# Block 2's second attention with negated scores: minima instead of maxima, and no sign change

## The reference, cut to what matters

```
scores = (q * 64 ** -0.5) @ k^T            # 128 queries a block, up to 512 local and 256 context keys
local  = where(valid, scores + bias, -1e30) # heads 0-7: a window, no bias; heads 8-15: a grid of neighbours, bias rpb
p      = softmax([sink,] context, local)    # the sink is one learned score of each head, in heads 0-7 only
out    = p @ v
```

## Time and profile before

| | us |
|---|---|
| three runs, median | 4175.17 |
| lowest, highest | 4165.76, 4179.91 |
| the profiled execution, its own time | 4163.56 |
| its span | 4161.8 |
| the paired attention, from the first `maximum` to the last diagonal product | 3487.3 to 3692.9 |
| PE, DVE, ACT, POOL busy in the span | 91%, 52%, 39%, 3% |

### The profile page before, as it was taken

How to read it: one execution, slowest core, us unless ns; L and a number is a source line. 1 busy time by engine, 2 the same in 40 slices (tenths; PEclk the granted TensorE clock), 3 DMA queues, 4 the chain that set the end, 5 groups by cost and what they waited for, 6 DMA issues and landing times.

```text
span 4161.8 us, 51828 instructions
## 1 busy us (share of the span) xinstructions
PE 3787.4 (91%) x18434; PEld 3096.5 (74%) x18434; DVE 2162.2 (52%) x3691; ACT 1602.3 (39%) x2423; POOL 137.4 (3%) x192
## 2 busy tenths in 40 slices
PE   7999988999999997999898876879999898998997
PEld 5788866877678875787577765768888677886885
DVE  4634456777653455777644555353333344755343
ACT  3233344332333344432353665442222234753222
POOL 0000000000000000000000000000000001410000
PEclk9999999999999998999898875899999999998999
DMA  3212323456221231345513300011212121112332
GB/s 120 91 61 81 106 66 101 144 153 202 71 87 60 90 113 51 122 146 172 159 46 68 30 0 0 26 41 61 66 61 65 45 66 45 19 45 66 96 96 71
DMA packets 114225, 333.81 MB, mean 80 GB/s; under 512 B 34479, under 2 KB 35247, under 8 KB 113455
## 3 DMA queue, kind: packets, MB, share of 16 engines
q1 hardware_dynamic: 83087, 269.06, 21.4%
q0 software_dynamic: 14400, 52.44, 4.2%
q10 hardware_dynamic: 16608, 10.61, 1.0%
HBM read 329.97 MB, written 6.97 MB: 81 GB/s over the span
## 4 chain that ended last, share of the span: by engine, by line
PE 80%; DVE 9%; ACT 5%; issue 2%; DVEq 2%; DMA 1%; POOL 1%; ACTq 0%; SPq 0%
PE PS L437 13%; PE PS L438 12%; PE PS L439 12%; PE PS L787 10%; PE PS L788 10%; PE PS L790 10%; PE PS L487 2%; PE PS L575 2%; PE PS L897 2%; PE PS L917 1%; PE PS L891 1%; PE PS L832 1%; PE PS L584 1%; PE PS L852 1%; DVE HVAL L1726 1%
## 5 line engine op out<-in xcount | busy, mean ns | idle before, releaser
L1682 DVE TENSOR_TENSOR WL<-RAW,WH 128x1024 fp32r<-128x1024 f32 x494 | 604.4, 1224 | 537.2 <-ACT WH L1082 533.4
L1082 ACT ACTIVATE WH<-RAW 128x1024 fp32r<-128x1024 f32 x494 | 521.3, 1055 | 680.3 <-PE PS L790 363.4
L437 PE MATMUL PS<-HHI,WH 128*128 128x512 f32 x1632 | 656.9, 403 | 42.2 <-DVE HLO L1719 37.0
L438 PE MATMUL PS<-HLO,WH 128*128 128x512 f32 x1632 | 643.7, 394 | 0.0
L439 PE MATMUL PS<-HHI,WL 128*128 128x512 f32 x1632 | 643.2, 394 | 0.0
L787 PE MATMUL PS<-H2HI,WH 128*128 128x512 f32 (+1 forms) x1464 | 525.7, 359 | 45.6 <-DVE H2LO L2131 35.8
L788 PE MATMUL PS<-H2LO,WH 128*128 128x512 f32 (+1 forms) x1464 | 496.1, 355 | 0.0
L790 PE MATMUL PS<-H2HI,WL 128*128 128x512 f32 (+1 forms) x1464 | 429.2, 354 | 0.0
L437 PEld LDWEIGHTS PS<-HHI,WH 128*128 128x128 f32 x1632 | 309.6, 190 | 131.2 <-issue 47.1
L787 PEld LDWEIGHTS PS<-H2HI,WH 128*128 128x128 f32 x1464 | 278.7, 190 | 120.5 <-issue 38.9
L439 PEld LDWEIGHTS PS<-HHI,WL 128*128 128x128 f32 x1632 | 309.8, 190 | 71.5
(11 more groups left out here) (333 smaller groups left out, 6266.0 us busy)
## 6 DMA issues: line engine op xcount, KB each, us to landing
RAW<-in_stream SPq DMA_DIRECT2D x494, 512.0 KB, 3.5
MODW<-in_modw POOLq DMA_DIRECT2D x96, 512.0 KB, 4.0
bias_rows<-in_rpb SPq DMA_DIRECT2D x1, 4762.5 KB, 55.0
MEM<-in_mem ACTq DMA_DIRECT2D x3, 1024.0 KB, 4.9
X<-in_x SPq DMA_DIRECT2D x1, 2048.0 KB, 9.3
CROW<-in_crow POOLq DMA_DIRECT2D x4, 512.0 KB, 4.5
out<-X SPq DMA_DIRECT2D x1, 2048.0 KB, 7.3
BIAS<-bias_rows ACTq DMA_DIRECT2D x8, 224.0 KB, 4.7
```

The lines of the kernel that those rows point to most:

```text
L437: nc.tensor.matmul(out, WH[:, slot, b * P:(b + 1) * P], hi, start=start, stop=False)
L438: nc.tensor.matmul(out, WH[:, slot, b * P:(b + 1) * P], lo, start=False, stop=False)
L1082: A(WH[:, d, :], RAW[:, s, :], ACT.Copy).then_inc(high_split, 1)
L1682: TT(WL[:, d, :], RAW[:, s, :], WH[:, d, :].bitcast(F32), ALU.subtract).then_inc(split_ready, 1)
```

## The change

Scores are carried with their sign changed. The queries of the last layer are scaled by -(64 ** -0.5) instead of 64 ** -0.5; the masks hold +1e30 for a forbidden key; the biases are subtracted from the mask where the mask was added to them; `maximum` takes minima, and starts from a negated sink (a new tile of 8 columns, filled once in block 2's prologue) or from +1e30; the exponential has the scale -1. The minimum of the negated scores is already what `exps` needs as bias, so the second `TTR` writes it where line 2199 wrote, line 2199 is gone, and the `drain` behind the second `TTR` now carries the semaphore. The instructions of the first block and of the first layer are as they were.

```diff
+        SINK = place2("SINK", [P, 8])
...
-                    nc.gpsimd.tensor_tensor(b, b, CMASK[:].unsqueeze(1).to_broadcast([P, DR, HD]), ALU.add).then_inc(grid_ready, 1)
+                    nc.gpsimd.tensor_tensor(b, CMASK[:].unsqueeze(1).to_broadcast([P, DR, HD]), b, ALU.subtract).then_inc(grid_ready, 1)
...
-                A(dst, FLAT[:, 3 * p * T:3 * p * T + TA].unsqueeze(1), ACT.Identity if scale else ACT.Copy, scale=HD ** -0.5 if scale else 1.0).then_inc(taken[p], 1)
+                A(dst, FLAT[:, 3 * p * T:3 * p * T + TA].unsqueeze(1), ACT.Identity if scale else ACT.Copy, scale=scale or 1.0).then_inc(taken[p], 1)
...
-                    A(p, p, ACT.Exp, bias=MX[:, 2 + h:3 + h], accum_out=DEN[:, h:h + 1]).then_inc(pair_exp, 1)
+                    A(p, p, ACT.Exp, bias=MX[:, 2 + h:3 + h], scale=-1.0, accum_out=DEN[:, h:h + 1]).then_inc(pair_exp, 1)
...
+            TS(SINK[:], SM[:, 4 * HD:4 * HD + 8], -1.0, None, ALU.mult)
             dve.drain().then_inc(lam_ready, 1)
...
-                        added, least = BAND[:, c:c + n - TC], SM[:, 4 * HD + j + 4 * h:4 * HD + j + 4 * h + 1]
+                        added, least = BAND[:, c:c + n - TC], SINK[:, j + 4 * h:j + 4 * h + 1]
...
-                    TTR(p[:, 0:n - TC], FLAT[:, c0:c0 + n - TC], added, 1.0, least, ALU.add, ALU.max, MX[:, 0:1])
+                    TTR(p[:, 0:n - TC], FLAT[:, c0:c0 + n - TC], added, 1.0, least, ALU.add, ALU.min, MX[:, h:h + 1])
                     dve.drain()
-                    TTR(p[:, n - TC:n], FLAT[:, c0 + T:c0 + T + TC], ZERO[:], 1.0, MX[:, 0:1], ALU.add, ALU.max, MX[:, 1:2])
-                    dve.drain()
-                    TS(MX[:, 2 + h:3 + h], MX[:, 1:2], -1.0, None, ALU.mult).then_inc(pair_max, 1)
+                    TTR(p[:, n - TC:n], FLAT[:, c0 + T:c0 + T + TC], ZERO[:], 1.0, MX[:, h:h + 1], ALU.add, ALU.min, MX[:, 2 + h:3 + h])
+                    dve.drain().then_inc(pair_max, 1)
...
-    band = np.concatenate([np.where(abs(jj - 3 * P - i) <= 128, 0, NEG), np.where((ck >= cs) & (ck < cs + 16), 0, NEG)], axis=1).astype(f4)
+    band = np.concatenate([np.where(abs(jj - 3 * P - i) <= 128, 0, -NEG), np.where((ck >= cs) & (ck < cs + 16), 0, -NEG)], axis=1).astype(f4)
```

More of the change, by code:

```diff
@@ L1603, in _ @@
                 for t, c in enumerate(IN_ORDER):
-                    take2(U2[:, c, :].unsqueeze(1), l and c in Q_CHUNK)
+                    take2(U2[:, c, :].unsqueeze(1), -HD ** -0.5 if l and c in Q_CHUNK else None)
                     if l == 0 and 3 <= t < 8:
@@ L2186, in maximum @@
                         c = (3 - qb + local[0]) * P
-                        added, least = BAND[:, c:c + n - TC], SM[:, 4 * HD + j + 4 * h:4 * HD + j + 4 * h + 1]
+                        added, least = BAND[:, c:c + n - TC], SINK[:, j + 4 * h:j + 4 * h + 1]
                     else:
-                        added, least = GRID_BIAS[j % 2][h][:, (6 - 2 * qb) * HD:(6 - 2 * qb) * HD + T], NEG
+                        added, least = GRID_BIAS[j % 2][h][:, (6 - 2 * qb) * HD:(6 - 2 * qb) * HD + T], -NEG
                         if qb == 0:
```

## The result

| | median us | lowest, highest | runs |
|---|---|---|---|
| before | 4170.82 | 4163.06, 4182.19 | 13 |
| after | 4187.80 | 4175.42, 4195.21 | 13 |

The ratio after to before is 1.0038 (95% interval 1.0027 to 1.0049): 17 us slower where 1.3 us faster, in effect no change, was forecast. The forecast set out from the median of three runs, 4175.17 us, 4.35 us above that of 13; from 4170.82 its sum would have given 4169.5, further off. The profiled execution of the changed kernel took 4188.95 us.

The account below looks back on a forecast made before the run. The prediction had PE bounding most of the span and the order of waits deciding the window half; -0.9 - 0.4 - 0.07 + 0.07 = -1.3 us, from 4163.56 to 4162.3, or 4173.9 against the median; range 4162 to 4183.

Parts of the forecast that it names:

- The rest: Outside the attention's main terms: minima, changed constants and the 32-byte move at 0, the negated sink's instruction at 0.07 us.
- Rival 4: The 32 bytes or the shift in time move something unseen by over 0.3% either way: 4160 or 4188; chance 0.09.
- The window half: Paired attention's band pairs, 3512 to 3588 us: 13 sign changes in the chain at 0.07 us each, 0.9 us gained.
- The ring: One band pair's chain: head 1's exponential, `inverse`, next `maximum`, line 2199, `turned_low`, `turned`, back to the exponential; 5.87 us a turn.
- The queue's wait: Ahead of `turned_low` in the band half: if line 2199's 0.07 us is this wait, which stays, the gain is 0.
- rival 1: Full latencies count: 0.15 us at 13 turns, another 0.15 for ACT's earlier start, 0.5 at the start; 4170.8 us, chance 0.14.
- The first pairs: Start of the paired attention, each sign change in series: 0.07 + 2 x 0.15 = 0.4 us gained (0.2 to 0.5).
- POOL's block: After the first pairs, POOL's mask additions hold DVE's one-column addition 1.59 us, so the next two visits gain nothing.
- The grid half: Paired attention, 3588 to 3693 us: PE decides, line 2199 is in the chain once, in the last pair; 0.07 us gained.
- rival 3: POOL pays for the repeated operand in first place at three places in the chain: 4186.3 us, chance 0.03.
- sink instruction: Added behind line 2095 of the prologue to negate the sink: costs 0.07 us (0 to 0.15).
- The distance over the stage: From the first `maximum` to the last diagonal product of the paired attention: 205.6 us, forecast to become 204.3.

Follow-up runs that it names:

- pad8: The kernel before plus an unused tile of 8 columns (32 bytes) where the change put its own: 4187.76 us against 4169.90, ratio 1.0042.
- after64: The changed kernel with its new tile made 64 columns wide (8 used): 4164.59 us against 4170.46 for the kernel before, ratio 0.9984.
- pad16: The kernel before plus an unused tile of 16 columns (64 bytes) where the change put its own: ratio 1.0035.
- pad56: The kernel before plus an unused tile of 56 columns (224 bytes) where the change put its own: ratio 1.0034.
- weights16: The kernel before with the weight tiles moved on by 64 bytes and everything behind them by 128: 4204.18 us, ratio 1.0076.
- all8: The kernel before with its whole memory, weights included, moved on by 32 bytes: ratio 1.0000.
- g_only: The kernel before with only GHI, GLO and Y2, the tiles of the MLP's second half, moved on by 32 bytes: 4176.00 us, ratio 1.0013.
- pad48: The kernel before plus an unused tile of 48 columns (192 bytes) where the change put its own: ratio 1.0010.

## Why the prediction was wrong

**The step that failed** stands in "The rest": "The new tile moves all that lies behind it in block 2 by 32 bytes; no row shows whether an address matters, and I take 0." It measured 17.9 us by itself (pad8), and it is the whole result. Rival 4 named it and gave it a chance of 0.09, with the right size (4188 for 4187.80), but on no ground, so that the size came true is luck; and the range, 4162 to 4183, left it out. That no row shows a thing was read as a reason for nought. It should have been bounded: block 2 takes 2086 of the 4162 us, so 1% on its matmuls' distance could be up to 21 us.

**The window half.** The ring was right, its worth less than half. In `turned_low`'s rows of the chain the same 12 turns take 70.14 us after (3533.91 to 3604.05) and 70.46 before (3513.89 to 3584.35): 5.845 us a turn against 5.872, so 0.03 us instead of 0.07, and over 13 turns 0.35 us instead of 0.9. The two starts show why: from the accumulator read to `turned_low` 0.12 us instead of 0.15. The queue's wait in front of `turned_low`, which the prediction named as the lower bound, was in part hidden under line 2199 and now shows. The full-latency rule of rival 1 is wrong here: the exponential of head 0 did start 0.2 us sooner, and the ring didn't shorten by it. Of the Trainium skill, "VectorE: DVE Perf Modes", the prediction used half of what the section "The DRAIN you can't avoid" says: it adds that a next operation which isn't held starts earlier, so the 0.07 us in the earlier trace rows isn't against it.

**The first pairs.** Pair 1's first reduction came 4.71 us behind the stage's first one, 4.91 before: 0.2 sooner, about as forecast. By pair 2's it was lost again (11.27 us, 11.24 before), and in after64, where PE has its full clock sooner, it is 10.61; pair 3's stands at 18.05 after, 18.53 before and 16.82 in after64, and at 17.2 in pad16, pad56 and weights16 with every sign change in place. From pair 2 on these times go with the clock rather than with the change. POOL's block stood as the prediction said, until POOL's two masks ended at 3530.72; the row after that answers to the earlier trace rows is

```profile
3529.09 1.65 DVE L2207 TENSOR_TENSOR DEN<-DEN,ES 128x1 f32<-128x1 f32 x1
```

What the prediction had wrong is that the clock had "no row that would change this": with D = 64 the clock's part was some 4 us, three times the sum.

**The grid half, POOL and the minima** came as forecast: 105 us, 2.11 us a mask (rival 3 is out), no price for a minimum. The prologue's sink instruction cost 0.07 us: it started at 2082.41 behind line 2096 at 2082.34. The distance over the stage, forecast at 1.3 us less, was 1.0 less in the two traces. That it came so near is in part luck: some 0.5 us of it is the sign change (0.2 in pair 1, 0.35 over the window half), and the same distance moves by up to 1.9 us between traces that all keep it.

**What stays open.** That the distance between weights and streamed activations counts is shown by seven sizes of gap (32, 64, 128, 192, 224, 256 and 512 bytes) and by weights16 and all8, and that the loss goes with the streamed tile by g_only. That it repeats after 256 bytes rests on the gaps of 256 and 512 bytes, both at D = 64. That it is PE's own two reads that meet, the load of the next weights and the stream, is what is left over and was not seen itself. ACT and DVE, which write the weight tiles, are not the other side: in 3810 to 4110 us the matmuls that started while both were idle followed each other at 0.2288, 0.2337 and 0.2267 us in the kernel before, pad8 and pad48, those during which a weight tile was being written at 0.2290, 0.2335 and 0.2267. Nor is it shown why D = 192 costs half as much in all as D = 96 with the same matmuls in the last layer (430), or why the change's gain shows at D = 64 alone. Between kernels with the same D the first layer's count still differs (569 and 575 at D = 128), and the first layer and the last rank D = 0 and 64 the other way round; none of this is explained.

## What to carry to other kernels

A new tile is an edit to every tile allocated behind it: give it room at the end, or pad it so that nothing moves, and judge a small change only after a run in which the addresses are those of before (here 8 unused columns cost 18 us, and the change itself was worth some 6 us at one distance and nothing that could be seen at three others). Where PE is busy all the time and still slower, count the matmuls in a fixed stretch; busy time can't show it. And a saving of a few tenths of a us in front of a stretch at the lower clock may be returned several times over, or not at all: look at the granted clock of both kernels there.

## What the runs showed of the hardware that was not expected

The distance in on-chip memory between the weight tiles and the streamed tiles sets how closely fp32 matmuls of 512 columns follow each other: 443 in 100 us at D = 0, 439 at 64, 430 to 432 at 32, 96, 128 and 192, 3% from end to end, at the full clock throughout. Moving all tiles together by 32 bytes changed nothing that could be measured (1.0000, 0.9991 to 1.0009).

The Trainium skill, "SBUF — State Buffer", section "Who interferes with whom", gives PE two independent read ports, one for the moving operand and one for the weight load, and says that only the port pair shared by DVE and GpSimd causes contention, PE never waiting on anyone. The runs show more than this: with every instruction the same, PE's matmuls were 2% slower or faster by the distance between what these two ports read (pad8, weights16, all8). The measurement decides, though which of the two reads waits was not seen; the shared pair's rule held as before (1.65 us above).
